# Value and memory-query projections of an attention stage cut into smaller pieces and laid over eight steps

## The reference, cut to what matters

```python
proj = h @ w_in + b_in                      # 1024 -> 2304
c_in, q, k, v, qm = jnp.split(proj, [s0, s1, s2, s3], axis=-1)
conv_out = conformer_conv(c_in, ...)        # depthwise, 31 taps, then a layer norm over 256 channels
diff_out = diff_attention(q, k, v, ...)     # 4 heads of width 128, two softmaxes each
mem_out  = memory_attention(qm, mem, ...)   # 4 heads of width 64, queries qm
mixed = jnp.concatenate([conv_out, diff_out, mem_out], axis=-1)
return mixed @ w_out + b_out
```

## Time and profile before

| what | us |
|---|---|
| median of 3 runs | 1488.17 |
| lowest and highest | 1485.2, 1488.5 |
| profiled execution, whole | 1487.39 |
| its span in the profile | 1485.5 |

### The profile page before, as it was taken

How to read it: one execution, slowest core, us unless ns; L and a number is a source line. 1 busy time by engine, 2 the same in 40 slices (tenths; PEclk the granted TensorE clock), 3 DMA queues, 4 the chain that set the end, 5 groups by cost and what they waited for, 6 DMA issues and landing times.

```text
span 1485.5 us, 22794 instructions
## 1 busy us (share of the span) xinstructions
PE 1429.4 (96%) x9771; PEld 1287.7 (87%) x9771; DVE 905.2 (61%) x1535; ACT 339.8 (23%) x714; POOL 108.2 (7%) x100
## 2 busy tenths in 40 slices
PE   6998999999999999999999998999999999999997
PEld 4866599999986679999989887988889998899986
DVE  3457478666274667868541398750678657666663
ACT  3126121100213422200054213434222101200010
POOL 2100011020000001112000000000000200010120
PEclk9999999999999999999999999999999999999999
DMA  8422266576423146765601531125335435155551
GB/s 285 156 88 105 106 235 218 211 270 214 155 97 113 57 170 238 268 214 201 215 24 57 166 118 57 61 71 171 113 114 171 169 115 171 59 170 171 171 177 50
DMA packets 125012, 222.47 MB, mean 150 GB/s; under 512 B 6105, under 2 KB 33009, under 8 KB 124657
## 3 DMA queue, kind: packets, MB, share of 16 engines
q1 hardware_dynamic: 123418, 218.33, 42.6%
q0 software_dynamic: 1184, 2.56, 0.6%
q10 hardware_dynamic: 311, 0.13, 0.0%
HBM read 218.91 MB, written 2.10 MB: 149 GB/s over the span
## 4 chain that ended last, share of the span: by engine, by line
PE 90%; DVE 6%; ACT 2%; DMA 1%; issue 1%; POOL 0%; SPq 0%; DVEq 0%; ACTq 0%
PE acc L1643 60%; PE scr L1643 14%; PE pvw L1643 7%; PE ptb L1643 2%; PE scr L1699 1%; PE ptb L1708 1%; PE pvw L2108 1%; PE scr L2100 1%; DMA tab<-in_rel_bias 1%; DVE big L1308 1%; PE ptb L1959 1%; DVE big L1341 1%; DVE big L1325 1%; PE acc L1668 0%; PE scr L2091 0%
## 5 line engine op out<-in xcount | busy, mean ns | idle before, releaser
L1643 PE MATMUL acc<-y,ring 128*128 128x256 f32 (+2 forms) x1360 | 254.7, 344 | 3.2 <-ACT y L782 2.4
L1643 PEld LDWEIGHTS acc<-y,ring 128*128 128x128 f32 (+1 forms) x1360 | 218.6, 192 | 29.2 <-issue 4.9
L1643 PE MATMUL acc<-x,ring 128*128 128x128 f32 (+1 forms) x960 | 160.2, 324 | 0.0
L1643 PEld LDWEIGHTS acc<-x,ring 128*128 128x128 f32 x960 | 144.6, 191 | 12.3 <-issue 1.0
L1643 PE MATMUL acc<-ring,big 128*128 128x256 f32 (+1 forms) x280 | 92.3, 479 | 0.0
L1643 PE MATMUL acc<-hid,ring 128*128 128x128 f32 x736 | 89.6, 276 | 1.3 <-DVE hid L1542 1.3
L1643 PE MATMUL acc<-ysq,ring 128*128 128x128 f32 (+1 forms) x592 | 84.7, 298 | 2.4 <-issue 2.4
L1643 PEld LDWEIGHTS acc<-hid,ring 128*128 128x128 f32 x736 | 85.6, 192 | 1.5 <-DVE hid L1542 1.5
L1643 PEld LDWEIGHTS acc<-ysq,ring 128*128 128x128 f32 x592 | 78.3, 192 | 6.0 <-issue 2.8
L1643 PEld LDWEIGHTS acc<-ring,big 128*128 128x128 f32 x280 | 52.5, 190 | 30.8 <-issue 26.9
L1050 DVE SCALAR_TENSOR_TENSOR ring<-ring,silc 128x512 f32<-128x512 f32 x84 | 71.1, 847 | 3.0
(11 more groups left out here) (415 smaller groups left out, 2552.0 us busy)
## 6 DMA issues: line engine op xcount, KB each, us to landing
ring<-in_w_in SPq DMA_DIRECT2D x24, 2048.0 KB, 8.7
ring<-in_w_up SPq DMA_DIRECT2D x16, 2048.0 KB, 7.8
ring<-in_w_down SPq DMA_DIRECT2D x16, 2048.0 KB, 8.3
ring<-in_ada_w SPq DMA_DIRECT2D x12, 2048.0 KB, 13.3
ring<-in_w_ffn_in SPq DMA_DIRECT2D x22, 1024.0 KB, 7.2
ring<-in_w_out SPq DMA_DIRECT2D x6, 2048.0 KB, 8.4
ring<-in_w_o_ssd SPq DMA_DIRECT2D x4, 2048.0 KB, 7.9
ring<-in_w_ffn_out SPq DMA_DIRECT2D x4, 2048.0 KB, 7.7
```

What stands on the lines that cost most here:

```text
L1643: ins = pe.matmul(dst, w, m, start=start, stop=stop, skip_group_check=True)
```

## The change

The work is the same; its place in the program and the shape of one part change.

- The value projection is cut into two halves of 256 columns ("pair" 0 and 1), each for both token halves: 32 matmuls of 128x256 instead of 16 of 128x512. Bank 8 then holds the values of heads 0 and 1 for all tokens, bank 9 those of heads 2 and 3. Pair 0, first tokens, is written ahead of the pipeline, before the wait for the keys (`ready(8)`); the other quarters follow in steps 0, 1, and 2 with 3.
- The memory queries are cut by half the contraction: four matmuls in each of the steps 4, 5, 6 and 7.
- The mean of the convolution goes from step 5 to step 3, its subtraction from VectorE's step 5 to step 4, the squares on ScalarE from step 6 to step 5, the mean square from step 7 to step 6 on TensorE and ScalarE. The multiplication stays in VectorE's step 8.
- Banks and `ready` counts follow.

```diff
@@ ScalarE
                 for k in range(STEPS + 2):
                     slot(k)
-                    if k < 2:
+                    if k in (0, 3):
+                        pair = k // 3
                         b = full()
-                        act.activation(v[:, 2 * k:2 * k + 2, :], b[:, :, :], ACT.Copy).then_inc(drained, 1)
-                    elif k < 4:
-                        b = full()
-                        biased(qmT[:, k - 2, :], b[:, 0, :], 14 + k).then_inc(drained, 1)
-                    elif k in (4, 6, 8, 10):
+                        act.activation(v[:, pair:pair + 3:2, :], b[:, :, :], ACT.Copy).then_inc(drained, 1)
+                    if k in (4, 6, 8, 10):
...
-                    if k == 5:
+                    if k == 3:
                         b = full()
                         act.activation(cst[:, 0, :], b[:, 0, :], ACT.Copy).then_inc(drained, 1)
-                    if k == 6:
+                    if k in (5, 7):
+                        pair = (k - 5) // 2
+                        b = full()
+                        biased(qmT[:, pair, :], b[:, 0, :], 16 + pair).then_inc(drained, 1)
+                    if k == 5:
                         act.wait_ge(csub, l + 1)
                         act.activation(csq, cy, ACT.Square).then_inc(csq_ready, 1)
-                    if k == 7:
+                    if k == 6:
                         b = full()
@@ VectorE
-                    if k == 5:
-                        dve.wait_ge(drained, done + 14)
+                    if k == 4:
+                        dve.wait_ge(drained, done + 11)
                         tt(cy, cy, over(cst[:, 0, :], 2), ALU.subtract).then_inc(csub, 1)
@@ TensorE
+                def value_part(b, w, pair, t, chunks=range(DC)):
+                    for k in chunks:
+                        ins = mm(b[:, t, :], x[:, k, t * P:(t + 1) * P], w[:, k, 256 * pair:256 * pair + 256], k == 0, k == DC - 1)
+                    return ins
+                def query_part(b, w, pair, chunks):
+                    for k in chunks:
+                        ins = mm(b[:, 0, :], w[:, k, pair * P:(pair + 1) * P], x[:, k, :], k == 0, k == DC - 1)
+                    return ins
+                wv = next_unit()
+                vb = free_bank()
+                value_part(vb, wv, 0, 0)
                 for k in range(STEPS + 2):
                     if k == 0:
                         ready(8)
                     if k == 2:
+                        ready(9)
+                    if k == 6:
                         ready(10)
                     if k == DIFF_STEPS - 1:
-                        ready(12)
+                        ready(13)
+                    if k == DIFF_STEPS + 1:
+                        ready(16)
                     slot(k)
...
+                    if k == 0:
+                        value_part(vb, wv, 0, 1).then_inc(filled, 1)
+                    elif k == 1:
+                        vb = free_bank()
+                        value_part(vb, wv, 1, 0)
+                    elif k == 2:
+                        value_part(vb, wv, 1, 1, range(0, DC // 2))
+                    elif k == 3:
+                        value_part(vb, wv, 1, 1, range(DC // 2, DC)).then_inc(filled, 1)
+                        to_release[0] += 1
                         pe.wait_ge(conv_done, l + 1)
...
+                    elif k == 4:
+                        wq = next_unit()
+                        qb = free_bank()
+                        query_part(qb, wq, 0, range(0, DC // 2))
+                    elif k == 5:
+                        query_part(qb, wq, 0, range(DC // 2, DC)).then_inc(filled, 1)
+                    elif k == 6:
                         pe.wait_ge(csq_ready, l + 1)
...
+                        qb = free_bank()
+                        query_part(qb, wq, 1, range(0, DC // 2))
+                    elif k == 7:
+                        query_part(qb, wq, 1, range(DC // 2, DC)).then_inc(filled, 1)
+                        to_release[0] += 1
```

## The result

| | before | after |
|---|---|---|
| median (lowest to highest) of 4 runs, us | 1488.34 (1485.2 to 1489.49) | 1464.75 (1463.68 to 1466.34) |
| profiled execution, us | 1487.39 | 1466.34 |
| its span, us | 1485.5 | 1464.4 |
| last key matmul to transposes of step 9, first layer | 49.69 | 38.39 |
| the same, second layer | 49.69 | 38.40 |

The ratio after to before is 0.9846, with a 95% interval from 0.9827 to 0.9864: 23.6 us (1.5%) off the median, and clear of the scatter. 1465.5 us had been forecast, in a range up to 1475 us.

A forecast was written before the change was run, and what follows sets the result against it. TensorE was taken as the bound, busy 1429.4 of 1485.5 us. Winning 11.15 us a layer, 22.3 in all, from 1487.4 gives 1465.1; with the median 0.8 us higher, 1465.5 was said, range from 4 us lower up to 1475.

The forecast's parts named there:

- The bound: Whole kernel: TensorE busy 1429.4 of 1485.5 us; time is won by less work there or by closing its gaps.
- The sum of work: Last key matmul to transposes of step 9: pieces sum to 38.3 us, stretch 38.54 instead of 49.69 us a layer.
- one gap of 0.27 us: Before the transposes of step 9: step 8 has no filler, so 0.27 us stays in place of 0.75.
- The opening: Before the first scores: a 3.46 us value quarter covers ScalarE's 1.92 us; the 2.01 us gap and low clock go.
- the low clock: TensorE at 1.2 GHz (granted clock 0.50), seen after both larger gaps of a layer's attention; expected to go with them.
- the 0.69 us wait for the values' copy: Placed in step 1: TensorE's wait for the copy of values just made, expected gone with a bank filled earlier.
- The middle: Steps 2 to 9: four-matmul filler makes 3.27 us against VectorE's 2.64 us chain; earlier subtraction leaves 0.9 us.
- The slack figures: TensorE arrives 0.9 us after VectorE at step 5's transposes (subtraction), and 0.9 us after ScalarE's squares.
- The weight loads: Added loads lie hidden under matmuls, 0.1 us a layer; rival: exposed, 5.7 us a layer, 1477 us, 3%.
- The clock: Attention of each layer: low clock costs 1.93 us at the opening and 1.52 us after the 2.84 us gap.
- the middle gap: TensorE's 2.84 us gap before the transposes of step 6, with 1.52 us of low clock behind it.
- The slower one: Rival: short pieces of steps 2 to 8, 25 us a layer, run at 1.2 GHz; 1515 us, 3%.

The follow-up runs named there:

- e2: Changed kernel without the opening: the first value quarter stands in step 0 with the second; 1472.09 us.
- e1: Kernel before with the opening alone: values in column halves, first quarter ahead of the wait for the keys; 1476.74 us, ratio 0.9921.
- e3: Kernel before with the convolution's statistics alone moved: mean to step 3, subtraction 4, squares 5, mean square 6; 1480.76 us, ratio 0.995.
- e4: Changed kernel with the convolution's statistics put back into steps 5 and 7, filler spread as in the change; 1475.32 us, ratio 0.9908.
- e5: Kernel before with the values in two column halves of 256 in their old steps, nothing else; 1489.92 us in one execution.
- e10: The kernel of e1 run once more, unchanged; 1482.27 us.
- e9: The kernel of e3 run once more, unchanged; 1478.79 us.
- e11: The changed kernel run once more, unchanged; 1466.95 us.
- e6: Changed kernel with the four query matmuls of step 5 moved to step 4, leaving step 5 without any; 1467.02 us.

## Why the prediction was right, point by point

*The bound.* Right: TensorE, with all its gaps of this kind in the two attentions. Removing the gaps removed the time and nothing took their place.

*The sum of work.* 38.3 us plus one gap of 0.27 us was forecast; 38.39 and 38.40 us with a gap of 0.27 us came. The rows now give 1.73 us for eight records of four value matmuls, as taken.

*The opening.* Right in size: e2 puts it at 3.98 us a layer with the low clock behind it (3.94 forecast from gap and clock), and e1 shows that it stands by itself. One slip of place: the 0.69 us wait for the values' copy stands at the start of step 2, not in step 1. It is gone as argued.

*The middle.* The forecast treated filler and statistics each as sound and gave the sum. e3 and e4 take them apart. Counted as stretch of the first layer, statistics alone win 2.45 us (47.24), filler alone with the opening 6.05 us (43.64), and both with the opening 11.30 us (38.39). The two need each other: without filler the steps fall to VectorE's pace, without the earlier mean the wait moves with the filler. In all three the low clock is counted in, as it came in these traces. The slack figures held. 0.9 us were forecast at the subtraction, 0.75 us measured; 0.9 us at the squares, 0.8 us measured.

*The weight loads.* The statement quoted from the Trainium skill (TensorE: Matmul & The Clock Gate, Part 3) would have given 1477. e5 shows 0.07 us a layer, and after the change TensorE has 34.03 us of loads beside 38.50 us of matmuls in 38.50 us. For these loads over all rows the measurement decides against it.

*The clock.* Right in sum, wrong in kind, and in part lucky. Of the 11.45 us a layer I gave 1.93 and 1.52 us to the low clock as if it belonged to the gaps. In the kernel before it did fall at all four gaps, in both traces. But e1 against e10 and e3 against e9 show that it may or may not.

Both terms were also too large for what a fall costs. One kernel with and without it differs by 1.69 us at the opening (e3, its two layers) and by 0.89 and 1.08 us at the middle gap (e10 against e1). For the opening, 0.16 us come from the reading: the 10.55 us run from a start in the timeline (87.32) to one in the chain (97.87), while the timeline has those scores at 97.71. e2 agrees: its 3.98 us less the gap of 2.05 and a restart of 0.26 (1.13 for 0.87, as in the forecast) leave 1.67 us for the clock. For the middle, I compared 3.50 us with 1.98 us of work without a wait; in e1, at full clock, the same pieces take 2.49 us (121.16 to 123.65), because TensorE waits 0.31 us for VectorE there. The low clock had hidden that wait. The sum holds all the same, since the change takes the wait away too.

So, as an estimate from these differences, 2.6 to 2.8 of the 11.3 us a layer are what the low clock costs on the occasions that it comes, and 8.5 to 8.7 us are the sure part. The change does away with the occasions. I left this out of the range. With falls that stay away in the kernel before, a single pair of executions can show 5 us less. The kernel before had one of 1482.85 us beside e11's 1466.95; whether the clock is why wasn't seen, since that one has no trace.

*The rivals.* None came. The slower one (short pieces at the low clock) is refuted by 1.00 over the whole stretch, in two traces.

## What to carry to other kernels

In a pipeline of short steps, work that nobody waits for should be cut to pieces that cover the wait, and put between the instruction that starts the other engine's chain and the one that needs its end; the same sum over the stage is not enough (e6). Where the other engine waits for something that this engine makes, filler ahead of that something moves both ends (e4); what helped here was an earlier place for it. And a stretch read from the trace between two fixed instructions separates 0.1 us, where totals of one kernel scatter by 3 us in a batch and by more between batches.

## What the runs showed of the hardware that I had not expected

The granted clock behind one and the same gap of TensorE is not fixed. In one kernel and one place, a gap of 2.83 us was followed once by 1.00 (e1) and once by 0.50 (e10), and a gap of 2.00 us once by 3.23 us for the first scores and once by 1.99 us (e3 and e9, first layer). Within e3 it differs between the layers. The Trainium skill (TensorE: Matmul & The Clock Gate, Part 1) says that the window of activity by which the clock is granted runs free and isn't reset when a kernel starts. A clock that differs from execution to execution behind one and the same gap is in keeping with that, but no run here shows the window, and what decides in a given execution stays open. Nor is it shown why the kernel before had the low clock at all four gaps in both of its traces.
